# One Trainium2 core, attention, convolution and product-key experts: high-part products ahead of the low part, one-hots on DVE and ACT, some low splits on POOL

## The reference, cut to what matters

```python
q = (h @ w_q).reshape(T, 8, 256)
s1 = einsum('thd,kd->thk', q[..., :128], k1); s2 = einsum('thd,kd->thk', q[..., 128:], k2)
v1, i1 = top_k(s1, 16); v2, i2 = top_k(s2, 16)
top, pos = top_k(all 256 sums v1 + v2, 16)        # idx = i1 * 128 + i2 at pos
g = softmax(top)
act = gelu(einsum('thkd,td->thk', u_tab[idx], h)) * g
out = einsum('thk,thkd->td', act, v_tab[idx])
```

## Time and profile before

| | us |
|---|---|
| runs shown | 2214.76, 2215.46, 2218.53 (median 2215.46) |
| profiled execution | 2214.98 |
| its span in the profile | 2213.2 |
| outside the span | 1.8 |

### The profile page before, as it was taken

The page is one execution under the profiler, slowest core; times in us unless marked ns, Lnnn a source line. Parts: engine busy times, 40 slices in busy tenths (PEclk is TensorE's granted clock), DMA queues, the critical chain, the costliest instruction groups (busy, mean ns, idle before and its releaser), DMA issues.

```text
span 2213.2 us, 29380 instructions
## 1 busy us (share of the span) xinstructions
PE 1899.6 (86%) x9774; PEld 1597.0 (72%) x9774; DVE 1585.7 (72%) x2557; ACT 844.2 (38%) x1207; POOL 530.3 (24%) x529
## 2 busy tenths in 40 slices
PE   5999999989999978866776777767999999999997
PEld 4888884359988877766776776766676766766765
DVE  4678997658789999974555454645777777777776
ACT  3012232035545444443433343433444444444444
POOL 0000000000000010038888788773011001001000
PEclk9999999989999999998888888888999999999999
DMA  8996657978756697775666566667888888888885
GB/s 356 420 411 243 223 221 286 401 283 313 277 189 222 218 332 260 254 261 200 230 232 238 210 234 227 231 217 270 324 321 312 321 318 320 326 313 325 325 316 192
DMA packets 135956, 618.02 MB, mean 279 GB/s; under 512 B 16049, under 2 KB 24785, under 8 KB 99025
## 3 DMA queue, kind: packets, MB, share of 16 engines
q1 hardware_dynamic: 105984, 464.57, 56.9%
q0 software_dynamic: 18496, 134.24, 17.1%
q10 hardware_dynamic: 11410, 18.36, 2.2%
HBM read 600.26 MB, written 16.79 MB: 279 GB/s over the span
## 4 chain that ended last, share of the span: by engine, by line
PE 41%; DVE 19%; POOL 12%; issue 9%; DMA 8%; ACT 8%; DVEq 1%; ACTq 0%; SPq 0%; POOLq 0%
PE ps L1320 10%; ACT w_hi L720 7%; DVE w_lo L365 6%; PE ps L990 6%; POOL oh L538 6%; POOL oh L537 5%; PE ps L1030 5%; PE ps L1192 4%; PE ps L1014 4%; DMA raw<-in_peer_v 3%; DVE big L1389 3%; DVE big L1826 3%; PE ps L1141 3%; PE ps L1041 3%; PE ps L1276 2%
## 5 line engine op out<-in xcount | busy, mean ns | idle before, releaser
L365 DVE TENSOR_TENSOR w_lo<-raw,w_hi 128x1024 fp32r<-128x1024 f32 x544 | 669.5, 1231 | 469.0 <-ACT w_hi L720 462.4
L720 ACT ACTIVATE w_hi<-raw 128x1024 fp32r<-128x1024 f32 x544 | 576.3, 1059 | 948.5 <-PE ps L992 467.1
L990 PE MATMUL ps<-a,w_hi 128*128 128x384 f32 x2048 | 649.5, 383 | 65.1 <-DVE w_lo L365 57.3
L992 PE MATMUL ps<-a,w_lo 128*128 128x192 f32 x2048 | 529.0, 258 | 0.0
L990 PEld LDWEIGHTS ps<-a,w_hi 128*128 128x128 f32 x2048 | 408.0, 199 | 92.0 <-DVE w_lo L365 65.9
L1320 PE MATMUL ps<-w_hi,a 128*128 128x512 f32 x1536 | 410.7, 403 | 52.7 <-DVE w_lo L365 40.6
L992 PEld LDWEIGHTS ps<-a,w_lo 128*128 128x128 f32 x2048 | 413.4, 202 | 0.2 <-issue 0.2
L1320 PEld LDWEIGHTS ps<-w_hi,a 128*128 128x128 f32 x1536 | 277.7, 189 | 164.3 <-DVE w_lo L365 101.0
L1320 PE MATMUL ps<-w_lo,a 128*128 128x512 f32 x1024 | 275.8, 391 | 0.0
L514 POOL DMA_INDIRECT big<-in_u_rows,row_ix x64 | 76.0, 1187 | 637.9 <-DMA row_ix<-big 388.3
L1320 PEld LDWEIGHTS ps<-w_lo,a 128*128 128x128 f32 x1024 | 192.8, 188 | 42.1
(11 more groups left out here) (226 smaller groups left out, 1821.0 us busy)
## 6 DMA issues: line engine op xcount, KB each, us to landing
raw<-in_peer_u SPq DMA_DIRECT2D x256, 512.0 KB
raw<-in_peer_v SPq DMA_DIRECT2D x256, 512.0 KB
early<-in_w_ada SPq DMA_DIRECT2D x60, 1024.0 KB, 10.8
early<-in_w_front SPq DMA_DIRECT2D x42, 1024.0 KB, 9.3
raw<-in_w_ada SPq DMA_DIRECT2D x20, 1024.0 KB, 10.7
raw<-in_peer_wq SPq DMA_DIRECT2D x32, 512.0 KB
big<-in_w_gate_f SPq DMA_DIRECT2D x16, 1024.0 KB, 5.2
raw<-in_w_front SPq DMA_DIRECT2D x14, 1024.0 KB, 8.8
```

The source lines that it names most:

```text
L365: engine.tensor_tensor(w_lo[:, s % 2, part], ring[j % ph.ring][:, part], w_hi[:, s % 2, part].bitcast(F32), ALU.subtract)\
L720: act.activation(w_hi[:, s % 2, :], ring[j % ph.ring], ACT.Copy).then_inc(hi_ready, 1)
L990: pe.matmul(ps[:, b % 2, 0:2 * TD].rearrange("p (m t) -> p m t", m=2), w_hi[:, half, cols], a_pair[:, kc, :, 0:TD], start=kc == 0, stop=Fa ...
L992: done = pe.matmul(ps[:, b % 2, 0:TD], w_lo[:, half, cols], a_hi[:, kc, 0:TD], start=False, stop=kc == KC - 1, skip_group_check=True)
```

## The change

1. Pattern letters: in UP and ROUTE every fourth unit, in MID 5 of 16, become "p": POOL makes these low parts (68 of 544 units).
2. PE: in each unit all products with the high part come first. They wait only for the rounding (`hi_ready`), and after them `hi_used` is raised; then PE waits for the low part and makes the products with it; after them `split_used` is raised. This holds in `product`, `query_blocks` and `down`.
3. ACT's rounding of unit s waits for `hi_used` and for the low part of unit s-2 (which reads `w_hi`), no longer for `split_used`. The low part of unit s waits for `split_used` of unit s-2 itself.
4. Masks: DVE makes the 8 one-hots of a group in one instruction of 1024 columns; ACT scales 4 of them (`scale_masks`). POOL makes none. The first group's place moves from 4 to 5.
5. POOL's queue holds low parts and gathers in order; the first three gathers come at place 4 of MID.

```diff
-PH_UP = Phase(PH_WQ, EXPERT_BLOCKS // 32, "w" * 16)
-PH_MID = Phase(PH_UP, EXPERT_BLOCKS // 32, "w" * 16)
-PH_ROUTE = Phase(PH_MID, EXPERT_BLOCKS // 16, "w" * 16)
+PH_UP = Phase(PH_WQ, EXPERT_BLOCKS // 32, "wwwp" * 4)
+PH_MID = Phase(PH_UP, EXPERT_BLOCKS // 32, "wwpwwpwwpwwpwwpw")
+PH_ROUTE = Phase(PH_MID, EXPERT_BLOCKS // 16, "wwwp" * 4)
...
-USE_FIRST, MASK_FIRST, PUT_FIRST = (5, 7, 9, 11, 13, 15), (4, 7, 9, 11, 13, 15), (7, 9, 11, 13, 15, 15)
+USE_FIRST, MASK_FIRST, PUT_FIRST = (5, 7, 9, 11, 13, 15), (5, 7, 9, 11, 13, 15), (7, 9, 11, 13, 15, 15)
...
         def low_part(engine, ph, j, i):
             s = ph.s + ph.nth(j)
             engine.wait_ge(hi_ready, at(i, ph.s_per, s + 1))
+            if s >= 2 or i is not None:
+                engine.wait_ge(split_used, at(i, ph.s_per, s - 1))
...
-            def make_masks(g):
-                if g == 0:
-                    gp.wait_ge(sel_made, 2)
-                else:
-                    gp.wait_ge(oh_used, g)
-                for t in range(4):
-                    token = slice(4 * g + t, 4 * g + t + 1)
-                    gp.tensor_scalar(masks[:, 0, t, :], iota[:, :], sel_T[:, 0, token], None, ALU.is_equal)
-                    done = gp.tensor_scalar(masks[:, 1, t, :], iota[:, :], sel_T[:, 1, token], sel_T[:, 2, token],
-                                            ALU.is_equal, ALU.mult)
-                done.then_inc(oh_ready, 1)
...
+            def work(ph, it, halves, row0):
+                for j in range(ph.per):
+                    if ph.pattern[j] == "p":
+                        low_part(gp, ph, j, it or None)
+                    if it == 0 and ph is PH_MID and j == 4:
+                        gp.wait_ge(gate_f_saved, 16)
+                        gp.wait_ge(row_ix_in, 32)
+                        for n in range(3):
+                            gather_next(n)
                     if j in halves[1::2]:
                         gather_next(row0 + halves[1::2].index(j) + 3)
...
                 act.wait_ge(landed[j % ph.ring], ph.landed(j, i))
                 if s >= 2 or i is not None:
-                    act.wait_ge(split_used, at(i, ph.s_per, s - 1))
+                    act.wait_ge(hi_used, at(i, ph.s_per, s - 1))
+                    act.wait_ge(*lo_before(ph, j, i, 2))
...
+            def scale_masks(g, i):
+                act.wait_ge(oh_masked, at(i, 6, g + 1))
+                for t in range(4):
+                    token = bass.ds(at(i, 24, 4 * g + t), 1)
+                    done = act.activation(masks[:, 1, t, :], masks[:, 1, t, :], ACT.Copy, scale=sel_T[:, 2, token])
+                done.then_inc(oh_ready, 1)
...
+                    pe.wait_ge(hi_ready, at(i, ph.s_per, s + 1))
+                    for k in range(UCH):
+                        kc = half * UCH + k
+                        done = pe.matmul(ps[:, b % 2, 0:2 * TD].rearrange("p (m t) -> p m t", m=2),
+                                         w_hi[:, half, k * P:(k + 1) * P], a_pair[:, kc, :, 0:TD], start=kc == 0,
+                                         stop=False, skip_group_check=True)
+                    done.then_inc(hi_used, 1)
                     for k in range(UCH):
                         kc = half * UCH + k
                         if k * steps % UCH == 0:
                             pe.wait_ge(unit_done[ph.pattern[place]],
                                        ph.done(place, i) - (steps - 1 - k * steps // UCH))
...
+            def make_masks(g, i):
+                if i is not None or g:
+                    dve.wait_ge(oh_used, at(i, 6, g))
+                dve.tensor_tensor(masks, iota[:, None, None, :].to_broadcast([P, 2, 4, P]),
+                                  sel_T[:, 0:2, bass.ds(at(i, 24, 4 * g), 4)].unsqueeze(3).to_broadcast([P, 2, 4, P]),
+                                  ALU.is_equal).then_inc(oh_masked, 1)
+
             def lo(ph, j, i):
-                low_part(dve, ph, j, i)
+                where = MASK if i is not None else MASK_FIRST
+                if ph is PH_ROUTE and j in where:
+                    make_masks(where.index(j), i)
+                if ph.pattern[j] == "w":
+                    low_part(dve, ph, j, i)
```

More of the change, by code:

```diff
@@ L356, in arrived, with lo_before @@
             return slot_in[n % SLOTS], 16 * (n // SLOTS + 1)
+        def lo_before(ph, j, i, back):
+            if j >= back:
+                return unit_done[ph.pattern[j - back]], ph.done(j - back, i)
+            if i is None:
+                before, place = ph.before, ph.before.per - back + j
+                return unit_done[before.pattern[place]], before.done(place, before.n - 1)
+            place = ph.per - back + j
+            steps = STEPS[ph.pattern[place]] * ph.each[ph.pattern[place]]
+            return unit_done[ph.pattern[place]], at(i, steps, ph.done(place, None) - steps)
         def low_part(engine, ph, j, i):
@@ L372, in slot_free @@
             def slot_free(ph, j, i):
[L374 to L380, removed]
-                else:
[L382 to L385, removed]
+                if j >= ph.ring or i is not None or ph.before:
+                    sp.wait_ge(*lo_before(ph, j, i, ph.ring))
             def bring(ph, i, w, block0=0, after=None):
@@ L515, in gather @@
                     .then_inc(done, 16)
-            gp.wait_ge(gate_f_saved, 16)
-            gp.wait_ge(row_ix_in, 32)
+            for it in range(PH_UP.n):
+                for j in range(PH_UP.per):
+                    if PH_UP.pattern[j] == "p":
+                        low_part(gp, PH_UP, j, it or None)
             v_rows = peer_v.rearrange("b p d -> (b p) d")
@@ L909, in _ @@
                     up_unit(PH_ROUTE, j, i)
-                    route(j, i, PUT)
+                    route(j, i, MASK, PUT)
             def high_group(g, i, made):
@@ L1188, in query_blocks, with part @@
                 k, banks = u % KC, (MIX_SECOND, MIX_FIRST)[u // KC]
+                def part(blk, w, a, m):
+                    return pe.matmul(ps[:, banks[blk // 2], (blk % 2) * T:(blk % 2 + 1) * T],
+                                     w[:, u % 2, blk * P:(blk + 1) * P], a[:, k, :],
+                                     start=k == 0 and m == 0 and blk % 2 == 0, stop=k == KC - 1 and m == 2,
+                                     skip_group_check=True)
+                pe.wait_ge(hi_ready, u + 1)
+                for blk in range(8):
+                    part(blk, w_hi, a_hi, 0)
+                    done = part(blk, w_hi, a_lo, 1)
+                done.then_inc(hi_used, 1)
                 pe.wait_ge(lo_ready, u + 1)
                 for blk in range(8):
[L1191 to L1195 removed]
+                    done = part(blk, w_lo, a_hi, 2)
                 done.then_inc(split_used, 1)
@@ L1314, in down @@
                         pe.wait_ge(at_lo, at(i, 2, j // 8 + 1))
-                    pe.wait_ge(lo_ready, PH_DOWN.done(j, i))
+                    pe.wait_ge(hi_ready, at(i, PH_DOWN.s_per, PH_DOWN.s + j + 1))
                     first, low, second = (a_down[:, blk, P:2 * P], a_down[:, blk, 0:P], a_down[:, blk, 2 * P:3 * P])
-                    for tt, a, w in ((0, first, w_hi), (0, low, w_hi), (1, second, w_hi), (0, first, w_lo),
-                                     (1, second, w_lo)):
+                    for m, (tt, a, w) in enumerate(((0, first, w_hi), (0, low, w_hi), (1, second, w_hi),
+                                                    (0, first, w_lo), (1, second, w_lo))):
+                        if m == 3:
+                            done.then_inc(hi_used, 1)
+                            pe.wait_ge(lo_ready, PH_DOWN.done(j, i))
                         for n in range(2):
```

45 lines of the change are left out of this document (17 added, 28 removed).

## The result

The changed kernel takes 2077.8 us in the median (2074.85 to 2085.03 in 4 runs) against 2215.16 (2214.76 to 2218.53 in 4 runs of the kernel before beside them): ratio 0.938, interval 0.936 to 0.941. It is faster by 137 us where 195 were forecast.

What follows compares the result with a forecast made beforehand. It took POOL's masks to bound ROUTE, DVE MID, DVE and PE nearly UP, and the loop over two places DOWN. ROUTE -135, DOWN -51, MID -5 and UP -4 make -195: 2215 to 2020 us, range 1945 to 2105.

Steps and rivals of the forecast that it cites:

- rival B: DOWN: transfers bound the phase and nothing is gained there; 2071 us in total, chance 0.20.
- PE's unit: UP, MID and ROUTE: 0.20 us from high product to low, 0.09 for low after low, 2.32 us a unit.
- the sum: ROUTE, per 16 units: DVE's 36.4 us, POOL's pieces 9.6, PE's waits 1.4 and semaphore gaps 3.2 make 50.6; -135 us.
- exclusion term: ROUTE: POOL's 8 low-part pieces of 1.2 us shut out DVE's two-operand instructions, adding 9.6 us per 16 units.
- meeting cost: MID: DVE meets POOL's pieces over half its time, losing 0.38 us a unit against 0.36 saved; phase -5 us.
- -4 forecast: UP: DVE's 0.29 us saved against 0.30 lost to POOL's pieces, PE waiting less at a unit's start; -4 us.
- I take 2.42: DOWN: with PE at 2.27 and transfers at 2.26 us, a unit takes 2.42 us; -51 us over 256 units.
- the bound of -80 at 2.31 us a unit: DOWN: the largest gain allowed for the phase, 80 us, if a unit takes 2.31 us.
- A: ROUTE: POOL's pieces cost DVE little and PE is the bound; -198 us for -135, 1957 us, chance 0.18.
- C: POOL's pieces take 2.4 us: ROUTE -70, MID +38, UP +23, DOWN -51; 2155 us, chance 0.10.
- D: POOL's low part paces 68 units; pieces of 3.6 us cost 224 us; slower than before, 2244 us, chance 0.05.
- E: Low after low product takes 0.13 us, PE's unit 2.6; UP and MID give back 8 us; 2028 us, chance 0.04.

Runs made afterwards that it cites:

- e1: The changed kernel with every low part back on DVE, none on POOL; 2026.1 us, ratio 0.915.
- e12: e5 with two of six groups of masks in ROUTE made one place earlier (5 and 13 for 6 and 14); 1949.4 us, ratio 0.881.
- e3: The kernel before with only the new order of products and waits; masks stay on POOL, all low parts on DVE; 2201.4 us, ratio 0.993.
- e5: e1 with DOWN written out without loops and 7 places for its units instead of 4; 1955.9 us, ratio 0.882.
- e6: Control for e5: the same text, DOWN written out, but with 4 places; 2031.7 us, ratio 0.916.
- e10: e5 with 5 places in DOWN instead of 7; 1971.0 us, ratio 0.890.
- e2: The kernel before with masks on DVE and ACT and the gathers' new place; all low parts on DVE, old order; 2062.5 us, ratio 0.930.
- e7: e2 (old order of products and waits) with DOWN written out and 7 places; 2057.9 us, ratio 0.927.
- e11: The changed kernel, POOL's low parts included, with DOWN written out and 7 places; 2000.7 us, ratio 0.903.
- e8: e1 with idle POOL subtractions of constants, read by nobody, at the 68 units whose low parts POOL made in the changed kernel; 2104.2 us, ratio 0.949.

## Why the time fell inside the range, and which steps failed

The range of 1945 to 2105 held, but of the 195 us forecast 137 came. ROUTE gave what was forecast, DOWN gave nothing of its 51 us, and MID lost 15. The nearest of the times on record was that of rival B, 2071.

**PE's unit: right, with two errors that cancel.** Two units of ROUTE in the changed kernel (PE's timeline), the first right behind mask products:

```profile
1378.39 1.63 PE L998 MATMUL ps<-a,w_hi 128*128 128x384 f32 x8
1379.86 1.03 PE L1007 MATMUL ps<-a,w_lo 128*128 128x192 f32 x8
1380.73 1.59 PE L998 MATMUL ps<-a,w_hi 128*128 128x384 f32 x8
1382.15 1.03 PE L1007 MATMUL ps<-a,w_lo 128*128 128x192 f32 x8
```

Eight high products take 1.47 us in the first unit and 1.42 in the second (0.178 each, the commonest value where PE does not wait), eight low ones 0.87 (0.109): 2.29 to 2.34 against 2.32 forecast. Low after low is not 0.09 but 0.109, and high after high not 0.20 but 0.178. The prediction had no row for the first and took the gap of another pair for it. The Trainium skill's section on LDWEIGHTS ("TensorE: Matmul & The Clock Gate") gives 0.107 us for such a load, and the measured 0.109 agrees; the 2.45 us for the unit, which the prediction worked out from it, were too long because the high products were quicker than its 0.20.

**ROUTE: the total right (-149 against -135), its working only in part.** An iteration takes 50.5 us where the sum had 50.6. That this is so close is partly luck, as DVE's busy time shows. e1, by phase:

```profile
586.00:756.00 170.00, 162.64 (x1081) 152.06 (x1082) 154.98 (x460) 92.16 (x146) 0.00 (x0) 1.00 0.68 221
757.00:956.00 199.00, 160.36 (x1027) 145.78 (x1025) 184.41 (x522) 83.91 (x129) 17.58 (x17) 0.99 0.80 271
956.00:1352.00 396.00, 354.97 (x2432) 350.29 (x2430) 344.12 (x458) 267.52 (x502) 74.80 (x51) 0.96 0.90 324
```

ROUTE of the changed kernel with the same borders:

```profile
973.00:1388.00 415.00, 360.09 (x2436) 354.26 (x2434) 356.27 (x428) 271.06 (x502) 174.45 (x115) 0.95 0.85 303
```

| us | UP | MID | ROUTE |
|---|---|---|---|
| DVE busy, e1 | 155.0 | 184.4 | 344.1 |
| DVE busy, after | 160.0 | 195.9 | 356.3 |
| low parts that DVE no longer makes, 1.22 each | 19.6 | 24.4 | 39.1 |
| so DVE's instructions became longer by | 24.6 | 35.9 | 51.3 |
| forecast for it | 19 | 24 | 77 |
| POOL's pieces, busy | 54.2 | 62.1 | 101.2 |

In each phase DVE loses about half of the time that POOL's pieces take, where the forecast took all of it in ROUTE and half of it, for shorter pieces, in the other two. In ROUTE 41 of the 51 us fall on the mask instructions (99.9 against 58.5). So the exclusion term was 6.4 us an iteration and not 9.6. A piece took 1.26 us at its shortest and 1.60 in ROUTE's mean, where 1.2 was forecast, so POOL bore a part of the exclusion too. The same sum without pieces, all 16 low parts on DVE, gives 41.0 + 4.6 = 45.6 us an iteration, 5.0 less; e1 takes 47.9 (six iterations, masks at 1008.83 and 1296.06), 2.6 less.

What made up for the oversized term were waits that the sum had at 1.4 + 3.2 us an iteration. In e1 (990 to 1340, some 7 iterations) PE waits for scaled masks:

```profile
PE ps L1299 <- ACT oh L839: 28.4, 17, 2.9
```

That is 4 us an iteration, about what lies between PE's own 43 to 44 (16 units of 2.29 to 2.34 and 6.4 for the masks) and the 47.9 that e1 takes; that this wait is the whole difference was not tried beyond e12, which took two of its places away for 7 us. In the changed kernel no engine is busy over 90% of ROUTE (DVE 352 of 408, PE 358). The forecast of DVE over 90% was wrong for that reason. A sum over one engine comes out right when another, nearly as long, stands behind it.

**MID: wrong sign (+15 against -5, inside its bounds of -35 to +40).** The failed step set DVE's saving of 0.36 us a unit against a meeting cost of 0.38, on the half of its time with two operands. By the table the meeting cost was 35.9 / 64 = 0.56 a unit: the pieces took 1.58 us in the mean and not 1.2, and DVE lost a little over half of that. The phase lost 12 us to it (e1). PE's busy time rose there from 160 to 171 us for the same products, at a granted clock of 0.92 instead of e1's 0.99. The order brought nothing here: MID is 199 to 201 us with it (e1, e3, e5, e6, e10, e12) and 196 to 200 in the old order (before, e2, e7).

**UP: -4 forecast, 0 measured.** The order is worth -7.5 (e3), where -4 was taken, and the pieces cost 7 (e1 to after), where their meeting with DVE was set equal to what DVE saves. It is the same mis-sized term as in MID: 24.6 us against 19.

**DOWN: -51 forecast, -3 measured.** The failed step is "I take 2.42", between PE's 2.27 and transfers' 2.26. The phase kept 2.61. Each of the two limits was within reach: with 7 places the same order gives 606 us, 82 less than before, all that the bound of -80 at 2.31 us a unit promised. What the sum left out was how many units may be under way. ACT's 44 us of waits for transfers in the earlier trace rows were the row that said so: a transfer came late at a share of 0.87, so it came late for another reason than a full load. Rival B gives the right size, but not for its reason: the transfer engines were not full. With 7 places the change itself comes to 2000.7 us (e11), below the forecast of 2020.

**Rivals.** A (POOL cheap) fails by e1 and e8, B gave DOWN's size, C and D (slow pieces) by the pieces' mean of 1.62 us, E (low after low 0.13) by its 0.109.

**Open.** With 4 places and the new order DOWN lies anywhere from 671 (e1) to 687 (e8), though the code of that phase is the same in several of them; what sets it was not found, and it makes 13 of e1's 52 us uncertain as a cost of POOL's pieces. One kernel alone can differ so from one execution to the next: e1 took 2025.6 to 2026.4 us three times and 2036.4 once, e6 2030.0 to 2031.9 four times and 2041.0 once, the one traced. How many us of e8's cost fall to DVE being held and how many to POOL's instructions being longer than the change's pieces (1.56 us for 384 columns, where a piece has 512 and 1.62) was not told apart.

## What to carry to other kernels

Before a wait is taken away, write down every loop that passes through the same buffers, with its length (places times unit time against transfer, conversion and use): the next longest is what the edit is worth against, and where two are equal only both edits together pay. A transfer that arrives late while the transfer engines' share is well below what they reach in another stretch asks for more places first, not for fewer bytes: here 7 places brought as much as leaving out 60 gathers (606 and 619 us). Beside a DVE full of two-operand instructions POOL may fill, but two-operand work moved to it is to be priced as time taken from DVE. Here half of POOL's time came out of DVE's, 112 us, more than the 83 us that DVE was spared.

## What the runs showed of the hardware

- A DVE instruction with two operands can stand through two POOL instructions in a row: 4.24 us for 1.22 of work, while POOL's two took 2.52.
- 136 POOL subtractions of 512 columns, 217.5 us in all, made DVE's instructions in the same phases 112 us longer.
- POOL's fills (0.42 us for 384 columns, 236 us of fills in all) cost DVE nothing measurable: 1223 ns for a low part against 1222 without them.
- A product of 384 columns is followed by another of its kind after 0.178 us and by one of 192 columns after 0.20; 192 after 192 takes 0.109.
- A transfer share of 0.89 with waits for transfers was latency over four places; the same queue with five carried 365 GB/s at 0.98.
